# A hybrid transformer block on one core: the short convolution moves from channels on the partitions to tokens on the partitions

## The reference, cut to what matters

```
h  = RMSNorm(x)
P  = h @ W_in                 # columns: u, B, C (1024 each), c_q, c_kv, k_rope
y_conv = B * causal_conv3(C * u, w)     # depthwise: y[t] = w2*v[t] + w1*v[t-1] + w0*v[t-2]
y_conv = RMSNorm over 8 groups of 128 channels
y_attn = latent attention over 8 heads, RMSNorm per head
x  = x + RMSNorm(concat(y_conv, y_attn) @ W_o)
x  = x + RMSNorm(relu(RMSNorm(x) @ W_up)^2 @ W_down)
```

## Time and profile before

| | |
|---|---|
| Median of 3 runs | 1072.35 us |
| The profiled execution | 1072.49 us |
| Its span in the trace | 1070.7 us |
| PE busy | 1055.3 us (99%) |
| DVE busy | 695.9 us (65%) |
| ACT busy | 514.4 us (48%) |
| Granted TensorE clock, mean | 0.998 of full |

### The profile page before, as it was taken

The page is one execution under the profiler, slowest core; times in us unless marked ns, Lnnn a source line. Parts: engine busy times, 40 slices in busy tenths (PEclk is TensorE's granted clock), DMA queues, the critical chain, the costliest instruction groups (busy, mean ns, idle before and its releaser), DMA issues.

```text
span 1070.7 us, 13495 instructions
## 1 busy us (share of the span) xinstructions
PE 1055.3 (99%) x4794; PEld 876.6 (82%) x4794; DVE 695.9 (65%) x781; ACT 514.4 (48%) x664; POOL 90.3 (8%) x102
## 2 busy tenths in 40 slices
PE   8999999999999999999999999999999999999996
PEld 7898888887878788888888888888888888888885
DVE  6475566679775777575565765756657556575666
ACT  6575545565444564444444444444444444444443
POOL 0011022100000610000000000000000000000003
PEclk9999999999999999999999999999999999999999
DMA  9786667863865465766656766666576665676562
GB/s 344 259 299 218 201 189 263 278 222 105 310 222 186 142 196 171 242 210 197 218 154 222 231 189 210 192 213 216 174 238 206 199 219 154 224 227 194 181 240 79
DMA packets 125619, 225.78 MB, mean 211 GB/s; under 512 B 8464, under 2 KB 30096, under 8 KB 124816
## 3 DMA queue, kind: packets, MB, share of 16 engines
q1 hardware_dynamic: 125152, 224.89, 64.4%
q10 hardware_dynamic: 432, 0.44, 0.1%
HBM read 210.08 MB, written 7.34 MB: 203 GB/s over the span
## 4 chain that ended last, share of the span: by engine, by line
PE 90%; DVE 7%; DMA 1%; issue 1%; ACT 1%; POOL 0%; SPq 0%; DVEq 0%; POOLq 0%; ACTq 0%
PE ps L721 30%; PE ps L723 29%; PE ps L722 29%; DVE w_lo L1294 3%; DVE conv_s L1521 1%; PE ps L744 1%; DMA raw<-in_w_in 1%; DVE conv_y L1509 1%; PE ps L905 0%; DVE conv_y L1522 0%; PE ps L910 0%; DVE xT_lo L1559 0%; ACT w_hi L999 0%; POOL x_res L1780 0%; DVE yT_lo L1525 0%
## 5 line engine op out<-in xcount | busy, mean ns | idle before, releaser
L1294 DVE TENSOR_TENSOR w_lo<-raw,w_hi 128x1024 fp32r<-128x1024 f32 (+2 forms) x382 | 467.3, 1232 | 322.3 <-ACT w_hi L999 320.4
L999 ACT ACTIVATE w_hi<-raw 128x1024 fp32r<-128x1024 f32 (+2 forms) x382 | 395.9, 1038 | 462.6 <-PE ps L723 459.6
L721 PE MATMUL ps<-w_hi,xT_hi 128*128 128x512 f32 (+1 forms) x792 | 308.7, 390 | 1.8 <-issue 0.6
L723 PE MATMUL ps<-w_lo,xT_hi 128*128 128x512 f32 (+1 forms) x792 | 306.1, 386 | 0.0
L722 PE MATMUL ps<-w_hi,xT_lo 128*128 128x512 f32 (+1 forms) x792 | 305.8, 386 | 0.0
L721 PE MATMUL ps<-w_hi,yT_hi 128*128 128x512 f32 x672 | 263.0, 391 | 2.0 <-DVE yT_lo L1328 1.7
L723 PE MATMUL ps<-w_lo,yT_hi 128*128 128x512 f32 x672 | 261.6, 389 | 0.0
L722 PE MATMUL ps<-w_hi,yT_lo 128*128 128x512 f32 x672 | 261.5, 389 | 0.0
L721 PEld LDWEIGHTS ps<-w_hi,xT_hi 128*128 128x128 f32 x792 | 148.7, 188 | 33.8 <-issue 3.2
L723 PEld LDWEIGHTS ps<-w_lo,xT_hi 128*128 128x128 f32 x792 | 148.7, 188 | 29.9
L722 PEld LDWEIGHTS ps<-w_hi,xT_lo 128*128 128x128 f32 x792 | 148.8, 188 | 28.7
(11 more groups left out here) (155 smaller groups left out, 432.0 us busy)
## 6 DMA issues: line engine op xcount, KB each, us to landing
raw<-in_w_up SPq DMA_DIRECT2D x64, 1024.0 KB, 5.5
raw<-in_w_down SPq DMA_DIRECT2D x64, 1024.0 KB, 5.3
raw<-in_w_in SPq DMA_DIRECT2D x28, 1024.0 KB, 5.6
raw<-in_w_o SPq DMA_DIRECT2D x16, 1024.0 KB, 5.2
aT_raw<-a_blk SPq DMA_DIRECT2D x240, 32.0 KB, 1.9
raw<-in_w_uq SPq DMA_DIRECT2D x8, 576.0 KB, 5.0
mix_rows<-blk SPq DMA_DIRECT2D x32, 128.0 KB, 2.4
raw<-in_w_ukv SPq DMA_DIRECT2D x4, 1024.0 KB, 5.4
```

Of the source, the lines that this page charges most:

```text
L721: nc.tensor.matmul(dst, x_hi, hi, start=first, stop=False)
L723: mm = nc.tensor.matmul(dst, x_hi, lo, start=False, stop=last)
L999: nc.scalar.activation(w_hi[:, slot, 0:size], raw[:, raw_slot, first:first + size], ACT.Copy).then_inc(hi_ready, 1)
L1294: nc.vector.tensor_tensor(w_lo[:, slot, 0:size], raw[:, raw_slot, first:first + size], f32(w_hi[:, slot, 0:size]), ALU.subtract).then_inc( ...
```

## The change

Both halves of the convolution (512 channels each) are now done with tokens on the partitions, on tiles of 128 x 1024 (2 token blocks x 512 channels).

- SP stores v = C * u of the half in a DRAM buffer `conv_rows` that begins with two rows of zeros (`store_u`), and reads it back twice, shifted by one and by two tokens, into parts of `lat` and of the rope tables (`read_u`).
- The taps are loaded from DRAM with the same row for all partitions into one buffer `conv_w` of three rows of 512 (`load_taps`): for half 0 beside quad 16, for half 1 behind `read_u(1)`.
- DVE does six whole-tile instructions (`conv_mix` 0 to 5): three products with taps, two adds, the product with B.
- ACT squares the tile, DVE sums over groups of 128 (`conv_stats`), POOL takes the power -0.5, DVE scales (`conv_scale`).
- DVE turns the result (`conv_turn`), SP moves the blocks, ACT and DVE write the high and low parts (`conv_split`).
- PE's 16 transposes and 8 products with ones for the convolution are gone. The first quad of output strip 0 waits for heads 0 to 3 alone.
- The loads of `x_res` and `g_post_mix` stand behind quad 56, no longer behind quad 50.

```diff
@@ plan(), between(sub)
-        if sub in (38, 54):
-            turn("conv", sub // 54)
...
-        for c in range(4):
-            for half, t, norm in [(0, 70 + 6 * c, 8), (1, 98 + 4 * c, 5)]:
-                if sub == t:
-                    steps.append(("convT", half, c))
-                if sub == t + 2:
-                    steps.append(("conv_square", half, c))
-                if sub == t + norm:
-                    steps.append(("conv_norm", half, c))
+        for h in range(2):
+            if sub == (34, 82)[h]:
+                shifts.append(("u_store", h, len(quads) + 4))
+            if sub == (64, 84)[h]:
+                shifts.append(("u_read", h, len(quads) + 4))
+            for op, when in enumerate([(50, 68, 70, 72, 74, 76), (86, 89, 91, 92, 94, 98)][h]):
+                if sub == when:
+                    steps.append(("conv_mix", h, op))
+            for when, what in [[(77, "conv_square"), (79, "conv_stats"), (82, "conv_scale"), (93, "conv_split")],
+                               [(99, "conv_square"), (100, "conv_stats"), (102, "conv_scale"), (111, "conv_split")]][h]:
+                if sub == when:
+                    steps.append((what, h, 0))
+            if sub == (84, 103)[h]:
+                turn("conv", h)
@@ SP
+            def load_taps(h):
+                for k in range(3):
+                    sp.dma_start(conv_w[:, k], t["conv_w"][0, k:k + 1, h * W:(h + 1) * W].to_broadcast([P, W])
+                                 ).then_inc(conv_w_landed, 16)
+            def store_u(h):
+                sp.wait_ge(strip_out_dve, h + 1)
+                sp.dma_start(conv_rows[h, 2:2 + SEQ].rearrange("(b p) n -> p b n", p=P), u_sb[:, h]
+                             ).then_inc(u_stored, 16)
+            def read_u(h):
+                sp.wait_ge(u_stored, 16 * (h + 1))
+                sp.wait_ge(zeros_stored, 16)
...
+                else:
+                    sp.wait_ge(ss_c_ready, h)
+                for back in (1, 2):
+                    sp.dma_start(shifted[back - 1], conv_rows[h, 2 - back:2 - back + SEQ].rearrange(
+                        "(b p) n -> p b n", p=P)).then_inc(u_shifted, 16)
+                if h:
+                    load_taps(h)
...
                 for m, (_, _, after) in enumerate(batches):
                     if after == n:
                         move_batch(m)
+                for what, h, after in shifts:
+                    if after == n:
+                        (store_u if what == "u_store" else read_u)(h)
@@ PE
-                elif what == "convT" and a == 1:
...
-                elif what == "conv_norm":
...
-                        if z["strip"] == S_OUT:
-                            pe.wait_ge(oT_lo_ready, PAIRS)
-                    if z["strip"] == S_OUT and z["q"] < 2 and k == 0:
-                        pe.wait_ge(convT_ready, 4 * z["q"] + 4)
+                    if z["strip"] == S_OUT and k == 0:
+                        if z["q"] < 2:
+                            pe.wait_ge(convT_ready, z["q"] + 1)
+                        else:
+                            pe.wait_ge(oT_lo_ready, 2 * z["q"] - 2)
@@ ACT
+                elif what == "conv_square":
+                    act.wait_ge(conv_mixed, 6 * a + 6)
+                    nc.scalar.activation(shifted[0], u_sb[:, a], ACT.Square).then_inc(conv_sq_ready, 1)
                     if a:
+                        nc.scalar.activation(std_m[:], ones[:, 0:TB], ACT.Sqrt)
+                elif what == "conv_split":
+                    act.wait_ge(blk_landed, landed(("conv", a)))
+                    for c in range(4):
+                        k = 4 * a + c
+                        ins = nc.scalar.activation(by_block(yT_hi[:, k]),
+                                                   conv_landed(a)[:, :, :, c].rearrange("p g b i -> p b g i"),
+                                                   ACT.Copy, scale=gains[:, G_CONV + k:G_CONV + k + 1])
+                    ins.then_inc(convT_hi_ready, 1)
@@ DVE
+                elif what == "conv_mix":
+                    u = u_sb[:, a]
+                    def tap(k):
+                        return conv_w[:, k].unsqueeze(1).to_broadcast([P, TB, W])
+                    dst, other, op = [(u, tap(2), ALU.mult), (shifted[0], tap(1), ALU.mult),
+                                      (shifted[1], tap(0), ALU.mult), (u, shifted[0], ALU.add),
+                                      (u, shifted[1], ALU.add), (u, b_sb[:, a], ALU.mult)][b]
+                    if b == 0:
+                        dve.wait_ge(conv_w_landed, 48 * (a + 1))
+                        dve.wait_ge(u_stored, 16 * (a + 1))
+                    elif b == 1:
+                        dve.wait_ge(u_shifted, 32 * (a + 1))
                     else:
+                        if b == 5:
+                            dve.wait_ge(strip_out_act, 5 + 2 * a)
+                        dve.wait_ge(conv_mixed, 6 * a + b)
+                    nc.vector.tensor_tensor(dst, dst, other, op).then_inc(conv_mixed, 1)
+                elif what == "conv_stats":
+                    dve.wait_ge(conv_sq_ready, a + 1)
+                    nc.vector.reduce_sum(ss_c[:], shifted[0].rearrange("p b (g n) -> p (b g) n", n=P), AX_X
+                                         ).then_inc(ss_c_ready, 1)
```

More of the change, by code:

```diff
@@ L76, in plan @@
 def plan():
-    steps, tail, quads, batches = [], [], {}, []
+    steps, tail, quads, batches, shifts = [], [], {}, [], []
     def quad(kind, n=None, **kw):
@@ L297, in plan @@
             tail.append((f"m_add_b{tb}", q, n))
-    return steps, tail, quads, batches
+    return steps, tail, quads, batches, shifts
 def hybrid_block(nc, t, out):
-    steps, tail, quads, batches = plan()
+    steps, tail, quads, batches, shifts = plan()
     BATCH = {(kind, i): n for n, (kind, i, _) in enumerate(batches)}
@@ L558, in hT_parts @@
             return [(2 * a + c, slice(0, SEQ), slice(c * SEQ, (c + 1) * SEQ)) for c in range(2)]
[L561 removed]
+        RESIDUAL_QUAD = min(n for n, z in quads.items() if z["kind"] == "out") + 8
         def turned(tile, at, tb):
@@ L930, in step @@
                     mm.then_inc(pv_done, 1)
-                elif what == "convT" and a == 1:
-                    pe.wait_ge(strip_out_dve, 2)
-                    pe.wait_ge(strip_out_act, 7)
-                    pe.wait_ge(o_ready, PAIRS)
-                    if conv_bank(a, b) == conv_bank(0, 0):
-                        pe.wait_ge(conv_std_ready, 4)
-                    transposes(conv_bank(a, b), [s[:, a, tb, b * P:(b + 1) * P] for s in (u_sb, b_sb)
-                                                 for tb in range(TB)]).then_inc(convT_filled, 1)
-                elif what == "conv_norm":
-                    i = 4 * a + b
-                    pe.wait_ge(ones_ready, 1)
-                    pe.wait_ge(conv_sq_ready, i + 1)
-                    if i == 0:
-                        pe.wait_ge(probsT1_ready, PAIRS)
-                    elif a == 0:
-                        pe.wait_ge(conv_std_ready, b)
-                    nc.tensor.matmul(ps[:, conv_bank(a, b), 0:SEQ], ones[:], conv_s[:, i % NCONV, :],
-                                     start=True, stop=True).then_inc(conv_sum_done, 1)
                 elif what == "hT":
@@ L1412, in step @@
                 elif what == "conv_turn":
-                    if a == 0:
-                        dve.wait_ge(strip_out_dve, 1)
-                    else:
-                        dve.wait_ge(strip_out_act, 5)
-                    src = (u_sb, b_sb)[a]
-                    turn_batch(b, [src[:, 0, tb].rearrange("p (c q i) -> p c q i", c=4, q=4) for tb in range(TB)])
+                    dve.wait_ge(conv_scaled, a + 1)
+                    turn_batch(b, [u_sb[:, a, tb].rearrange("p (c q i) -> p c q i", c=4, q=4) for tb in range(TB)])
                 elif what == "lat_split":
@@ new lines, in step @@
+                elif what == "conv_mix":
[10 more added lines that the diff above has]
+                        dve.wait_ge(u_shifted, 32 * (a + 1))
+                    else:
+                        if b == 5:
[6 more added lines that the diff above has]
+                                         ).then_inc(ss_c_ready, 1)
+                elif what == "conv_scale":
+                    dve.wait_ge(rstd_c_ready, a + 1)
+                    u = u_sb[:, a].rearrange("p b (g n) -> p (b g) n", n=P)
+                    nc.vector.tensor_tensor(u, u, rstd_c[:].unsqueeze(2).to_broadcast([P, 8, P]), ALU.mult
+                                            ).then_inc(conv_scaled, 1)
+                elif what == "conv_split":
+                    dve.wait_ge(convT_hi_ready, a + 1)
+                    for c in range(4):
+                        k = 4 * a + c
+                        for tb in range(TB):
+                            ins = split_blocks(yT_hi[:, k], yT_lo[:, k], conv_landed(a)[:, :, tb, c], G_CONV + k, tb)
+                    ins.then_inc(convT_ready, 1)
@@ L1728, in step @@
```

(5 more changed lines are left out.)

117 lines of the change are left out of this document (40 added, 77 removed).

## The result

The changed kernel takes **1089.99 us** (median of 4, 1089.52 to 1090.60) beside 1072.41 us of the kernel before on the same chip: a ratio of 1.0166 (95% interval 1.0153 to 1.0179), +17.6 us. The forecast was 1084.7, its range ended at 1090.0. The profiled execution took 1090.37 (+17.9 against that of before), with a span of 1088.5 and a mean granted clock of 0.988.

The account below looks back on a forecast made before the run. PE, busy 99% of the span, was taken as the bound. New PE waits of 20.9 us less 8.8 removed gave 12.1; on 1072.49 the forecast was 1084.7 us, own range 1082 to 1088, wide range 1079.5 to 1090.

Parts of the forecast that it names:

- R: Landing of half 1's reads and taps, last in SP's chain of DMAs: forecast 274.8, taken as 274.6.
- half 95: Quad 47, steps 2 and 3: PE waits 15.6 us while DVE stands until R.
- values product: PE's wait at 236.77 for the last probabilities: 0.8 us, or 2.3 if half 0's reads land 1.5 later.
- half 98: PE, ready at R + 10.6, waits 1.8 us until R + 12.4 because of DVE's queue.
- half 103: Sum over groups, POOL, scale and turn between w_lo's bring it 0.8 us late.
- What goes, 8.8: PE products with ones and transposes, 5.2 us, plus waits, 3.6; 1063.7 if nothing new came late.
- The first read: Half 0's reads, 1 MB behind the kqT load of 218.64, land at 225.1; DVE waits 2.4 us.
- The turn of the heads: DVE's turn of the last heads moves from 250.1 to 253.0: 0.7 more DVE work, 2.2 idle for ACT.
- The clock: After the long wait PE starts half 95 at 1.2 GHz; losses up to 3.8 us are covered, cost taken as 0.
- Quad 54: First quad to need convolution half 1: starts at R + 41.8 = 316.4 instead of 304.2, +12.2 us.
- longer, or the clock stays low: Rival: slower store and reads put R at 281, 1091 us, or the clock costs 4.3, 1089; chance 0.15.
- The faster rival: Half 1's conv_mix 0 finds its taps landed, R below about 259: 1065.1 us; chance 0.05.

Follow-up runs that it names:

- the run of 1063.3: Changed kernel with half 1's taps loaded early, v's store ahead of the heads' move, reads before the heads' load, and both halves' DVE steps respread: 1063.33 us.
- the run with early taps: Changed kernel with half 1's taps in a place of their own, loaded behind quad 47, nothing else moved: 1083.21 us.
- the run with 74 products: Changed kernel with 74 products of 128x128 with ones keeping PE busy in the long gap before half 95: 1090.94 us, beside 1090.56 of the changed kernel.
- The run without the norm: Changed kernel without the second group norm's rstd on POOL; half 1 scaled by half 0's, so wrongly: 1086.95 us.
- the run with the round trip first: Changed kernel with half 1's store of v, reads and taps issued ahead of the block moves at quad 49: 1078.77 us.
- the interleaved one: Changed kernel with half 1's taps loaded behind quad 47, v's store ahead of the heads' blocks, reads between the heads' stores and their load: 1073.08 us.

## Why the prediction was wrong in size and right in its mechanism

Three terms of the sum failed. Two lie in the chain to R, the landing of half 1's rows and taps: v's store, taken as 3.8, took 4.96, and the reads with the taps, taken as 6.8, took 8.05. The third is what lies behind R: POOL's norm, taken as 1.4, took 2.8, and the half clock behind the wait it makes, put at nothing, took 1.6.

The direction and the place held: a wait of PE before half 95, made by DVE standing at the first conv_mix of half 1 until taps and rows are there. The terms, in us lost by PE:

| term | predicted | measured |
|---|---|---|
| values product | 0.8 | 1.8 |
| half 94 | 0.6 | 0.4 |
| half 95 | 15.6 | 17.1 |
| half 98: wait / half clock in its place | 1.8 | 2.2 |
| half 101 | 1.2 | 0.7 |
| half 103 | 0.8 | 2.1 |
| second half clock | 0 | 1.6 |
| small ones and rest | 0.1 | 0.8 |
| sum | 20.9 | 26.7 |
| removed | -8.8 | -8.8 |
| total | +12.1 | +17.9 |

(Measured ones are gaps between starts less 0.23, from the rows above; what is removed is measured by the run of 1063.3, which has no wait left; the rest is what the total of the profiled execution leaves.)

- **What goes, 8.8.** Right: without late arrivals the time is 1063.3, forecast 1063.7.
- **The first read.** It landed at 226.04, forecast 225.1 by the earlier trace rows: 0.9 late, and the values product 1.0 later than forecast. "If the reads land 1.5 later it is 2.3" was the right slope.
- **The turn of the heads.** 253.43 against 253.0: right, with ACT's square in front of a w_hi as its largest part.
- **R, the step on which the forecast rested.** The load of the convolution's blocks was issued at 264.00 (forecast 263.8). Two terms behind it were too small. v's store took 4.96 until the reads went out (264.38 to 269.34), where I had taken 3.8 between bounds of 2.6 and 6.1. The reads and taps took 8.05 (269.34 to 277.39), where I had taken 6.8 between 5.0 and 10.7. With 0.2 from upstream and 0.2 rounded off, R is 277.39 instead of 274.6. I had taken for the store the duration of a load with 0.5 for what lay ahead of it, though the nearest row by position, the MB behind another load, said 6.1. For the reads I had used the slope of two large loads; but one MB alone already took 5.6 in the run with early taps, and in the changed kernel the reads land 5.6 after 269.34 too, the taps 2.4 later. Why the store takes longer than a load of its size no run tests; it took more, 6.1 to 7.2, where a 1 MB load stood ahead of it. Nor did the rows say that little of a DMA shrinks with size: 3.3 us for 512 KB and 5.0 for 1 MB leave 1.6 fixed, as an estimate. The Trainium skill, "DMA: Bandwidth & Descriptors", section "Anatomy of one DMA", gives its fixed part and rate for DMAs issued by GpSimd, and these are SP's, which the prediction passed over. As an estimate by that page the two terms are 3.2 and 6.2, further off than the rows; the measurement decides.
- **PE's wait.** R + 2.4 is right to 0.1 (279.81). The wait grew by only 1.5 of the 2.8, because PE came to half 95 1.3 later than forecast.
- **Behind R.** Half 98: no wait, because the half clock took its place, as the cover in the prediction says; the run with 74 products shows both the wait and the equal time. Half 103: POOL's norm takes 2.8 on 8 columns, and I took 1.4, the wait for the 4-column norm. 0.6 of the difference is the power on twice the columns, a plain omission; 0.9 is the multiplication beside DVE's w_lo. The run without the norm measures it with what follows it, 3.0. The listed parts up to "half 1 ready" also add up to R + 37.7 and not 37.9; measured it is ready at 316.60, R + 39.2.
- **The clock.** Cost 0 was right for the long gap. The Trainium skill, "TensorE: Matmul & The Clock Gate", section "Why this matters for your kernels", has the half rate come back after a long gap, and the trace agrees (1.00 before, 0.50 from 270 on). The second fall, behind a wait of 2.0, was not foreseen and lies where nothing covers it.
- **Quad 54** starts at 322.24 instead of 316.4, 5.8 late: 2.8 of it are R, and 3.0 lie behind R, 1.3 of them at half 103 and 1.6 in the second half clock. "At R + 45 or later the load on DVE behind it was under-counted": it is R + 44.9, and the under-counted load was POOL's and the clock's, not DVE's.
- **The rivals.** The time is that of "longer, or the clock stays low" (1089 to 1091), but by neither of its two ways, R at 281 or 4.3 us of clock behind the long gap. The faster rival's condition, R below 259, was met only by moving the round trip in front of the chain; that gave 1073.1, and with the spread 1063.3.

The likeliest case's own range, 1082 to 1088, missed the time. The wide one ends where the time lies: 1090.0 is 1.0165 times the 1072.35 of the kernel before, and the measured ratio is 1.0166. That it ends so near owes to how far the neighbouring cases reach, and not to the sum. I had let the unknown terms of the chain vary one against another about their middles; both moved up, and the terms behind R had no spread of their own at all.

## What to carry to other kernels

When a change adds a trip through DRAM, write down the issuing queue's whole chain in front of it: here the computation was worth -8.8 us and the waits around it +26.7; reordering the issues, with a second place for the taps, won 16.9 of them, and spreading DVE's steps behind that 9.8. Start such a trip before whatever only becomes ready later, and give the tile that lands last its own place. Then spread the consumer's steps between the other work of its engine; a wait that looks small may only be hidden by a longer one ahead of it. Size every term for the shape that it will have, the columns of a small POOL instruction among them, and look at what DVE does beside it.

## What the runs showed of the hardware that was not expected

- Raising to a power on POOL: 1.64 us on 128x8 where it was 1.01 on 128x4.
- The multiplication before it on POOL: 1.10 us on 128x8 where a w_lo of DVE ran beside it, 0.20 on the same shape where DVE stood idle.
- The 512 KB store to DRAM took 4.9 us here behind the 512 KB load, 6.1 in the run with the round trip first, 6.4 in the interleaved one and 7.2 in the one of 1063.3, each behind a 1 MB load; in the kernel before the one at the end took 2.6.
- Waits of some 2 us were followed by a half clock in four profiles of eight.
